# Expert steps of 64 or 32 rows, and weights held behind the first row load, in a two-layer mixture-of-experts backbone

## What is computed

```python
s = jax.nn.sigmoid((t @ w_router).astype(F32))
sel = s + b_router.astype(F32)
...
_, eidx = lax.top_k(jnp.where(emask, sel, -jnp.inf), TOP_K)      # 2 experts a token, inside the best of 4 groups
...
for e in range(N_EXPERTS):
    y = (jax.nn.silu(t @ w_gate[e]) * (t @ w_up[e])) @ w_down[e]  # 1024 -> 512 -> 1024
    out = out + combine[:, e:e + 1] * y
```

## Time and profile before

| | |
|---|---|
| median of the runs | 1699.07 us (1694.97 to 1700.27) |
| the profiled execution, its own time | 1703.08 us |
| its span | 1700.9 us |
| granted TensorE clock, mean | 0.932 |
| busy: TensorE, its weight loads, DVE, ACT | 84%, 52%, 42%, 29% |
| mean rate of the DMA engines | 230 GB/s |
| TensorE's gate and up matmuls (L1667) | 349.6 us |
| TensorE's down matmuls (L1680) | 176.9 us |
| first and last gate and up matmul, layer 0 | 594.1 and 943.1 us (the last is the extra loop's) |
| the same, layer 1 | 1399.2 and 1659.7 us |

### The profile page before, as it was taken

The page is one execution under the profiler, slowest core; times in us unless marked ns, Lnnn a source line. Parts: engine busy times, 40 slices in busy tenths (PEclk is TensorE's granted clock), DMA queues, the critical chain, the costliest instruction groups (busy, mean ns, idle before and its releaser), DMA issues.

```text
span 1700.9 us, 18561 instructions
## 1 busy us (share of the span) xinstructions
PE 1430.4 (84%) x7346; PEld 881.8 (52%) x7346; DVE 722.5 (42%) x1120; ACT 496.2 (29%) x683; POOL 50.9 (3%) x50
## 2 busy tenths in 40 slices
PE   5899999999997099899999577889999818889784
PEld 3678777678774033333333256788789602223221
DVE  4865667665453411111111167687777341111012
ACT  4843345351524000000000047545556300000000
POOL 0000000000030100000000100000001000000000
PEclk9999999999999599999999777999999859999997
DMA  9685652222200688878989565644324069999994
GB/s 347 244 341 216 261 198 99 100 75 95 79 27 1 237 274 313 307 291 335 371 316 376 177 222 213 237 149 149 115 109 149 27 203 379 392 383 394 402 421 162
DMA packets 64457, 390.54 MB, mean 230 GB/s; under 512 B 9072, under 2 KB 11316, under 8 KB 24852
## 3 DMA queue, kind: packets, MB, share of 16 engines
q1 hardware_dynamic: 45786, 343.10, 53.1%
q10 hardware_dynamic: 14490, 29.36, 5.4%
q0 software_dynamic: 4096, 16.91, 2.7%
HBM read 365.48 MB, written 47.97 MB: 243 GB/s over the span
## 4 chain that ended last, share of the span: by engine, by line
issue 43%; PE 37%; DVE 9%; ACT 5%; DMA 3%; POOL 2%; ACTq 0%; POOLq 0%; DVEq 0%; SPq 0%
PE bank L1384 8%; PE bank L1386 8%; PE bank L1385 8%; DVE wlo L860 2%; PE bank L1416 2%; PE bank L1417 2%; ACT whi L540 1%; PE bank L1362 1%; POOL m_lo L506 1%; PE bank L1594 1%; DMA stage<-in_mod 1%; ACT L540 1%; DMA hrow_d<-in_hy_bias 1%; PE bank L1572 1%; PE bank L1397 1%
## 5 line engine op out<-in xcount | busy, mean ns | idle before, releaser
L1667 PE MATMUL bank<-wexp,xg 128*64 128x512 f32 x1504 | 349.6, 609 | 54.3 <-DMA wexp<-in_expert 50.8
L860 DVE TENSOR_TENSOR wlo<-stage,whi 128x2048 fp32r<-128x2048 f32 x104 | 240.4, 2320 | 56.4 <-ACT whi L540 54.7
L1667 PEld LDWEIGHTS bank<-wexp,xg 128*64 128x64 f32 x1504 | 102.6, 139 | 267.0 <-issue 189.6
L1384 PE MATMUL bank<-h_hi,whi 128*128 128x512 f32 (+1 forms) x640 | 223.8, 350 | 9.8 <-DVE h_lo L860 7.7
L540 ACT ACTIVATE whi<-stage 128x2048 fp32r<-128x2048 f32 x104 | 197.7, 1904 | 79.3 <-PE bank L1386 42.8
L1385 PE MATMUL bank<-h_lo,whi 128*128 128x512 f32 (+1 forms) x640 | 219.0, 342 | 0.0
L1386 PE MATMUL bank<-h_hi,wlo 128*128 128x512 f32 (+1 forms) x640 | 218.8, 342 | 0.0
L1680 PE MATMUL bank<-wexp,act_a 128*64 128x512 f32 x752 | 176.9, 614 | 6.4 <-DVE act_a L860 6.4
L540 ACT ACTIVATE yrow<-bank 128x512 f32<-128x512 f32 x47 | 28.1, 597 | 502.4 <-PE bank L1680 489.0
L1306 DVE COPY gu_sb<-bank 128x512 f32<-128x512 f32 x47 | 32.5, 692 | 309.5 <-PE bank L1667 309.5
L1384 PEld LDWEIGHTS bank<-h_hi,whi 128*128 128x128 f32 x640 | 123.4, 193 | 31.0 <-DVE h_lo L860 8.9
(11 more groups left out here) (247 smaller groups left out, 1670.0 us busy)
## 6 DMA issues: line engine op xcount, KB each, us to landing
wexp<-in_expert SPq DMA_DIRECT2D x192, 1024.0 KB, 15.4
stage<-in_mod SPq DMA_DIRECT2D x48, 1024.0 KB, 6.3
stage<-in_in SPq DMA_DIRECT2D x40, 1024.0 KB, 4.9
xpick<-x_rows ACTq DMA_DIRECT2D x49, 256.0 KB, 9.5
y_rows<-yrow ACTq DMA_DIRECT2D x94, 128.0 KB, 6.6
x_rows<-in_c_zero SPq DMA_DIRECT2D x23, 512.0 KB, 6.5
y_rows<-in_c_zero SPq DMA_DIRECT2D x23, 512.0 KB, 7.6
stage<-in_out SPq DMA_DIRECT2D x8, 1024.0 KB, 4.9
```

Source lines behind the costliest of these rows:

```text
L860: return V.tensor_tensor(o, x, y, op)
L1384: MM(o, w[0], x_[0], start=start, stop=False)
L1667: ins = MM(bank[0][h * C:(h + 1) * C, :], xg[:, kk, :], wexp[:, z, j, c], start=(kk == 0), stop=(kk == KT - 1))
```

## The change

The plan's capacities are counted in half steps of 32 rows. A step of a rank takes 64 rows, or 32 where only 32 are left of its capacity. The capacities fall with rank now to 256, 256, 224, 128, 96, 96, 64, 64, 64 and six times 32 rows in layer 0 (before: 256 three times, 128 three times, 64 nine times) and to 128, 128, 96, 64, 64, 64 and nine times 32 in layer 1 (before: 128 three times, 64 twelve times). The number of steps stays 27 and 18, nine and ten of them of 32 rows, and the order is a new one.

A step of 32 rows (w = 32, n = P // w = 4) uses four groups of 32 output partitions. In `gate_up` the 16 matmuls are the same in number and in moving columns (512 each), but the even and the odd piece of the input width add up in different groups. The two sums are added in `turn`, where four ordinary matmuls with a constant matrix `halves` take the place of the four transposes. In `down` each of the four groups makes a quarter of the output width, with 16 matmuls of 256 columns for eight of 512. Rows are loaded by 32, and the result is stored in four pieces of 32 rows x 256 columns, under one semaphore `y_out` that counts 64 a step.

At L466 SP waits no longer for the scattered rows but for the landing of the first row load (`xload0`), which ACT issues when the rows are scattered.

```diff
@@ -7,17 +7,18 @@
 
 
 C = 64
-CAPS = ((4, 4, 4, 2, 2, 2) + (1,) * 9, (2, 2, 2) + (1,) * 12)
-ORDER = ((1, 1, 1, 1, 13, 5, 5, 2, 9, 12, 2, 4, 4, 10, 2, 8, 2, 6, 0, 0, 7, 11, 0, 14, 0, 3, 3),
-         (6, 0, 0, 11, 7, 2, 2, 5, 13, 3, 1, 1, 4, 8, 10, 12, 9, 14))
+HALF_STEP = 32
+CAPS = ((8, 8, 7, 4, 3, 3, 2, 2, 2) + (1,) * 6, (4, 4, 3, 2, 2, 2) + (1,) * 9)
+ORDER = ((3, 3, 4, 4, 1, 11, 1, 1, 1, 0, 10, 0, 14, 0, 13, 0, 7, 5, 5, 12, 2, 2, 6, 2, 2, 8, 9),
+         (14, 11, 0, 0, 12, 7, 13, 5, 9, 6, 4, 1, 8, 1, 2, 2, 3, 10))
...
+        assert sorted(order) == [r for r, n in enumerate(caps) for _ in range((n + 1) // 2)] and len(caps) == experts - 1
+        self.bases = [sum(caps[:r]) * HALF_STEP for r in range(experts)]
...
-            c = rows.get(r, 0)
-            rows[r] = c + 1
-            self.steps.append((z, uses[z], filled[r], self.bases[r] + c * C))
+            row = rows.get(r, self.bases[r])
+            wide = min(C, self.bases[r] + caps[r] * HALF_STEP - row)
+            rows[r] = row + wide
+            self.steps.append((z, uses[z], filled[r], row, wide))
...
+    halves = np.zeros((128, 64))
+    for g in range(4):
+        halves[32 * g:32 * g + 32, 32 * (g // 2):32 * (g // 2) + 32] = np.eye(32)
...
-        "plan": np.broadcast_to(np.concatenate([np.array([[n * C for n in caps] + [-1], p.bases]).ravel() for caps, p in zip(CAPS, plans)])[None, :], (128, 64)),
+        "halves": halves, "plan": np.broadcast_to(np.concatenate([np.array([[n * HALF_STEP for n in caps] + [-1], p.bases]).ravel() for caps, p in zip(CAPS, plans)])[None, :], (128, 64)),
...
-        "x_moe", "y_hy", "y_out0", "y_out1", "zf0", "zf1",
+        "x_moe", "y_hy", "y_out", "zf0", "zf1",
...
+        def per_tile(buf, n, w):
+
+            return buf[:, 0:n * w].rearrange("p (k n) -> p k n", k=n)
...
@@ -463,7 +472,7 @@
                     for j in range(EC):
                         if r == plan.loads[0] and j == 3:
 
-                            sp.wait_ge(S("scattered"), 2 * (T // P) * 16)
+                            sp.wait_ge(S("xload0"), 16)
...
-                    row = places[s]
-                    act.dma_start(xpick[:, s % XR, :], x_rows[row:row + C, :]).then_inc(S(f"xload{s % XR}"), 16)
-
-                def silu(s):
+                    row, w = places[s]
+                    act.dma_start(xpick[0:w, s % XR, :], x_rows[row:row + w, :]).then_inc(S(f"xload{s % XR}"), 16)
...
-                    fn(yrow[:, :], bank[3][:, :], ACT.Copy).then_inc(S("y_ev"), 1)
+                    gate_cols = per_tile(bank[2], 4, 2 * w)[:, :, 0:w]
+                    fn(per_tile(act_s, 4, w), gate_cols, ACT.Silu).then_inc(S("silu"), 1)
+
+                def y_out(s, row, w):
+
+                    n = P // w
+                    fn(yrow[:, 0:w * 8], bank[3][:, 0:w * 8], ACT.Copy).then_inc(S("y_ev"), 1)
                     act.wait_ge(S("y_ev"), s + 2)
-                    for h in range(2):
-                        act.dma_start(y_rows[row, h * 512:(h + 1) * 512], yrow[h * C:(h + 1) * C, :]).then_inc(S(f"y_out{h}"), 16)
+                    for h in range(n):
+                        act.dma_start(y_rows[row, h * 8 * w:(h + 1) * 8 * w], yrow[h * w:(h + 1) * w, 0:w * 8]).then_inc(S("y_out"), 64 // n)
...
-                            for h in range(2):
-                                act.wait_ge(S(f"y_out{h}"), (s - 2) * 16)
-                        y_out(s - 2, slice(row_, row_ + C))
+                            act.wait_ge(S("y_out"), (s - 2) * 64)
+                        y_out(s - 2, slice(row_, row_ + w_), w_)
...
                     dve.wait_ge(S("xT_mm"), s + 1)
-                    V.tensor_copy(xg[:, :, :].rearrange("p k n -> p (k n)"), bank[1][:, :]).then_inc(S("xg"), 1)
+                    V.tensor_copy(xg[:, 0:KT * w], bank[1][:, 0:KT * w]).then_inc(S("xg"), 1)
...
                     dve.wait_ge(S("silu"), s + 1)
-                    up_cols = bank[2][:, :].rearrange("p (k n) -> p k n", k=4)[:, :, C:2 * C]
-                    tt(act_a[:, :, :], act_s[:, :, :], up_cols, MUL).then_inc(S("act_a"), 1)
...
+                    up_cols = per_tile(bank[2], 4, 2 * w)[:, :, w:2 * w]
+                    tt(per_tile(act_a, 4, w), per_tile(act_s, 4, w), up_cols, MUL).then_inc(S("act_a"), 1)
...
-                def columns(b):
+                def columns(b, w):
                     for k in range(KT):
-                        ins = T_(bank[1][:, k * C:(k + 1) * C], xpick[:, b, k * P:(k + 1) * P], C)
+                        ins = T_(bank[1][:, k * w:(k + 1) * w], xpick[0:w, b, k * P:(k + 1) * P], w)
...
-                def gate_up(s, z, fill):
-
+                    columns(s % XR, plan.steps[s][4])
+
+                def gate_up(s, z, fill, w):
+
+
+                    n = P // w
+                    x_ = per_tile(xg, KT, w)
                     pe.wait_ge(S("xg"), s + 1)
                     for j in range(4):
                         pe.wait_ge(S(f"ew{z}{j}"), fill * 16)
                         for k in range(2):
-                            kk = 2 * j + k
                             for h in range(2):
+                                g = h if n == 2 else 2 * h + k
+                                first_, last_ = (2 * j + k, 2 * j + k - 7) if n == 2 else (j, j - 3)
                                 c = slice((2 * k + h) * 512, (2 * k + h + 1) * 512)
-                                ins = MM(bank[0][h * C:(h + 1) * C, :], xg[:, kk, :], wexp[:, z, j, c], start=(kk == 0), stop=(kk == KT - 1))
+                                ins = MM(bank[0][g * w:(g + 1) * w, :], x_[:, 2 * j + k, :], wexp[:, z, j, c], start=(first_ == 0), stop=(last_ == 0))
                         ins.then_inc(S(f"used{z}{j}"), 1)
...
-                def down(s, z, fill):
-
+                def down(s, z, fill, w):
+
+                    n = P // w
+                    a_ = per_tile(act_a, 4, w)
                     pe.wait_ge(S("act_a"), s + 1)
                     pe.wait_ge(S("y_ev"), s + 1)
                     for j in range(2):
                         pe.wait_ge(S(f"ew{z}{4 + j}"), fill * 16)
                         for k in range(2):
                             kk = 2 * j + k
-                            for h in range(2):
-                                c = slice((2 * k + h) * 512, (2 * k + h + 1) * 512)
-                                ins = MM(bank[3][h * C:(h + 1) * C, :], act_a[:, kk, :], wexp[:, z, 4 + j, c], start=(kk == 0), stop=(kk == 3))
+                            for h in range(n):
+                                c = slice(k * D + h * 8 * w, k * D + (h + 1) * 8 * w)
+                                ins = MM(bank[3][h * w:(h + 1) * w, 0:8 * w], a_[:, kk, :], wexp[:, z, 4 + j, c], start=(kk == 0), stop=(kk == 3))
                         ins.then_inc(S(f"used{z}{4 + j}"), 1)
...
-                def turn(s):
+                def turn(s, w):
...
                     for k in range(4):
-                        ins = T_(bank[2][:, k * P:(k + 1) * P], gu_sb[:, k * P:(k + 1) * P])
+                        tile = gu_sb[:, k * P:(k + 1) * P]
+                        if w == C:
+                            ins = T_(bank[2][:, k * P:(k + 1) * P], tile)
+                        else:
+                            ins = MM(bank[2][:, k * 2 * w:(k + 1) * 2 * w], tile, halves[:, :], start=True, stop=True)
                     ins.then_inc(S("aT"), 1)
...
-                for s, (z, use, fill, row) in enumerate(plan.steps):
-                    gate_up(s, z, fill)
+                for s in range(STEPS):
+                    gate_up(*step(s))
                     if s + 1 < STEPS:
                         step_columns(s + 1)
                     if s > 0:
-                        down(s - 1, *(plan.steps[s - 1][i] for i in (0, 2)))
-                    turn(s)
-                down(STEPS - 1, *(plan.steps[STEPS - 1][i] for i in (0, 2)))
+                        down(*step(s - 1))
+                    turn(s, plan.steps[s][4])
+                down(*step(STEPS - 1))
```

69 lines of the change are left out of this document (32 added, 37 removed).

## The result

The changed kernel takes **1636.66 us** (median of 4 runs, 1633.28 to 1639.61) against 1699.67 (4 runs, 1694.97 to 1704.31) for the kernel before on the same chip: a ratio of 0.9629, 95% interval 0.9594 to 0.9664, 63.0 us less. The forecast was 1649.6, with a range of 1627 to 1684: right in sign, inside the range, and 13 us too cautious (of the forecast's own narrower range, 1636 to 1664, the time meets only the lower edge).

The account below looks back on a forecast made before the run. It took TensorE to bound layer 0, with the queue close behind, and transfers to bound layer 1. Layer 0's -41.5 and layer 1's -8 sum to -49.5, from the median of 1699.07 to 1649.6 us; range 1627 to 1684.

Parts of the forecast that it names:

- The narrow step: TensorE's 32-row step, four records at a time: 7.03 us against 11.83, 4.8 us less each.
- rivals B: Narrow matmuls: records run at 0.79 of four at a time; 1662 us, chance 0.08.
- C (two at a time): Narrow matmuls: records still run in pairs, a narrow step takes 12.2 us; 1694 us, chance 0.13.
- D (one): Narrow matmuls run one after another, a narrow step takes 22.5 us; 1859 us, chance 0.05.
- rival A: The y buffer or ACT's four stores set the beat, every narrow step 9.9 us; 1676 us, chance 0.11.
- this row as a sign that it would be wrong: ACT's yrow copies found waiting for the stores would show the forecast wrong; no size given.
- the first step starts 3 us earlier: Start of both layers: first row load takes 3.7 us, not 6.9; 3 us gained in layer 0, 0 in layer 1.
- I keep these and add 5: Layer 0's waits for weights: the 22.7 us stay and the new order adds 5.
- some 48 us to spare: Layer 0's weight queue before the change: some 48 us of slack, yet 22.7 us of waits occur.
- I take 0.6 us of 1.62: Layer 1: rows in and out of a narrow step cost 0.6 us less, nine steps, -5.4 of that layer's -8.
- Rival E: The new order also removes layer 0's waits, and rows are halved in full; 1620 us, chance 0.05.
- F: A capacity is exceeded, so the extra loop runs again, about 20 us; 1670 us, chance 0.04.

Follow-up runs that it names:

- a_order3: The changed kernel with a third order of steps in layer 0; 1618.06 us, ratio 0.9521.
- a_old_hold: The changed kernel with the fourth chunk waiting for the scattered rows again, not the first row load; 1637.70 us, ratio 0.9636.
- b_hold: The kernel before with only the new wait, the fourth chunk waiting for the first row load; 1694.14 us, ratio 0.9974.
- b_new_order: The kernel before with only the new order of steps, in both layers; 1687.73 us, ratio 0.9931.
- a_hold5: The changed kernel with the wait for the first row load ahead of the sixth chunk, not the fourth, in both layers; 1635.11 us, ratio 0.9617.
- c_l1_old: The changed kernel with a third order of steps in layer 0 and the order of the kernel before in layer 1; 1613.67 us, ratio 0.9510.
- a_l1_wide: The changed kernel with all steps of layer 1 at 64 rows; 1657.09 us, ratio 0.9757.
- a_old_order: The changed kernel with the order of steps of the kernel before, in both layers; 1663.30 us, ratio 0.9786.

## Why the prediction was right, and where it was not

**The narrow step** was right, and with it the sign and most of the size. 7.03 us forecast; measured 3.57 + 0.60 + 1.86 + 1.03 = 7.1. Four records at a time, the value taken from the pair that costs nothing, is what the rows show, and rivals B (three-tile rule, 8.3 us), C (two at a time) and D (one) are out. The Trainium skill (TensorE: Matmul & The Clock Gate, the speedup table of Part 3) stops at three column tiles, 2.38 times one, which is 0.79 of the ideal. For four tiles of this f32 form the trace gives the full factor, 32 records in eight beats of 0.43 us; the measurement decides here.

**What lies beside it.** The y buffer and ACT's four stores (rival A) were rightly counted at nothing, but not because nobody waits. ACT's waits in layer 0's stage, 584 to 876:

```profile
ACT yrow L549 <- DMA y_rows<-yrow: 53.0, 8, 7.8
```

The prediction had named this row as a sign that it would be wrong, and that was too strict: a wait on ACT counts only when TensorE comes to need what stands behind it. a_order3 shows it. From 585 to 853 ACT waits there 11 times for its stores,

```profile
ACT yrow L549 <- DMA y_rows<-yrow: 80.8, 11, 8.7
```

and TensorE's steps meet their sum without waits to 0.2 us.

**The first row load.** Landing after 3.6 us in layer 0 was right (3.7 forecast). The step that failed is "the first step starts 3 us earlier", carried into the sum as 3 us of the end: a_old_hold has it at nothing in layer 0. It would have needed the question asked of every other term, what is late next: the first wait for weights. Layer 1, taken as 0, has 0.5 to 1.6. For the kernel before by itself (b_hold) the 3 us may be true.

**The waits of layer 0** are the mis-sized term and most of the miss: "I keep these and add 5" gave 27.7 us, measured are 17.6. I had listed the experts that the new order wants early, and did not work out what it does for all the others. b_new_order shows that by itself: with all steps wide its first gate and up start at 595.48 and its last planned step at 906.22, where 595.48 + 10.53 + 25 x 11.83 = 901.8 is the sum without waits, so the 22.7 us have become 4.5. And these waits are not a fixed sum to be kept: narrow steps raise them, to 49.1 in the old order, the new order lowers them, and 17.6 is what both leave. The reasoning that a slot is refilled only once its last step has used it was right; it should have been worked through step by step for both orders. So layer 0 in full: start 3.3 earlier, eight narrow steps at 4.73 (37.8), the end from the last planned step to the extra expert 19.99 to 15.66 (4.3, one of its products in part at the lower clock), waits 5.1 less: 50.5. Forecast -41.5, with 41.4 for start and steps (measured 41.1), 5.1 for the end (4.3) and +5 for the waits (-5.1). One number behind that reasoning was off as well: the queue's "some 48 us to spare" come out as 43 with today's rows (85 x 2.67 + 26 x 1.62, 1.4% of it overlapping, from 592 on, against 900.4); nothing in the sum uses it.

**Layer 1** came out at -8.8 for -8, and that is in part luck. The end, behind the last quarter of the last planned step (1646.42 before, 1580.85 after), is 2.7 us shorter, as forecast. Up to that quarter the stage is 6.2 us shorter (250.2 us after the first row load, 256.4 before), where I had 5.4 for lighter rows. But two things I didn't have lie in these 6.2. Narrow steps in the old order bring 10.5 there (245.8 us, with the hold), because a row load half as large saves 0.7 us, more than the 0.6 of "I take 0.6 us of 1.62" for the load and the stores together; and the new order gives 4.4 back in the hole of the queue, which I had not looked for in layer 1 at all. That its pace goes by what its queues carry was right. The kernel before, 1390 to 1660, has

```profile
DMA packets 17329, 104.92 MB, mean 389 GB/s; under 512 B 2293, under 2 KB 2293, under 8 KB 5683
...
q10 hardware_dynamic: 4237, 9.44, 10.8%
```

and the changed one 101.12 MB at the same rate. Of these 3.80 MB, 2.65 are rows (9.44 to 6.79), 6.8 us; the other 1.2 are weights, of which both kernels load the same; the longer window only takes in more of them at its edges, an effect and not a cause. That the mean rate is the same is chance too: in the old order, without the hole, the narrow steps run at 396.

**The sum.** -49.5 forecast, -63.0 measured by the medians, -59.3 by the stages. Rival E (the waits vanish as well, 1620) had the mechanism that carried the miss; the order that makes it true exists, and stands at 1618. F is out: one run of the extra loop remains.

## What to carry to other kernels

When steps that cover a load are made shorter, the order of the steps is worth as much as the shortening: here 21 us of narrow steps and 17 of order made 50 together, and another order 18 more. Ask of every microsecond saved at the start which wait stands first behind it. And in a stage that its queues set, count what all of them carry, the small transfers at more than their bytes, and look for holes in the bandwidth row. A wait costs more than its idle time where the clock falls behind it: here 49 us for 33 idle.

## What the hardware showed that I had not expected

Weights put ahead of the scatter cost it their own time. Its eight stores are issued 1.27 us apart and land 1.27 us apart, so a backlog that stands ahead of the first of them is never worked off, and two more chunks make all eight land 4 to 5 us later. The stretch from the first chunk to the first row load grew by 5.1 and 4.4 us in a_hold5, and with one chunk less than c_l1_old it shrank by 0.8 and 3.3. It follows that idle-looking time ahead of a scatter is not free for weights.

In layer 1 TensorE's granted clock was lower with narrow steps. In 1341 to 1580 it is 0.85 (the third window at the top), where the earlier trace rows have 0.99 and a_l1_wide, 1340 to 1580, has 0.98:

```profile
1340.00:1580.00 240.00, 194.46 (x944) 65.53 (x942) 27.46 (x47) 14.70 (x30) 0.00 (x0) 0.98 1.00 385
```

What TensorE did in that stretch of the changed kernel, 1335 to 1581:

```profile
PE bank L1677 <- DMA wexp<-in_expert: 51.7, 36, 3.8
```

The waits alone don't explain it: a_l1_wide has 45.4 us of them in 37 pieces in its window and keeps 0.98. In this stretch the lower clock costs next to nothing, since the chunks set the pace. Where TensorE sets it, it costs: in a_old_order's layer 0 some 11 us by estimate (49.1 less 32.7 idle, less 0.2 for each of 25 quarters that start anew), and at the end of the changed kernel's layer 0 the narrow down at 885.56, behind a wait of 2.55 us, took 2.94 us instead of the 1.93 of 639.28, at a granted clock of 0.64.
